# A decoder step on one core: seven products of constants behind the last squares of each residual stage

## The chip, the core and the metric

The kernel runs on one core of one Trainium2 chip. The metric is the device time of one execution in microseconds (us), the median of several runs. The profile is of one further execution of the same program. TensorE does the matrix products and writes PSUM, VectorE and ScalarE do elementwise work and read PSUM, GpSimd copies small edges, and SyncE issues the loads of weights. Engines run on their own and meet at semaphores.

## The reference

One step of a 4-layer decoder with width 1024 in fp32, for a prompt of 512 tokens and 8 samples of 8 tokens each; the kernel holds all 576 tokens side by side. The mixers of the four layers are a (RWKV-7 time mixing), b (forgetting attention), c (short gated convolution) and a again. Cut to the frame:

```
def rmsnorm(x, g):
    y = xf * lax.rsqrt(jnp.mean(xf * xf, axis=-1, keepdims=True) + RMS_EPS)
    return (y * g.astype(jnp.float32)).astype(x.dtype)

for i in range(DEPTH):                      # DEPTH = 4
    hp, hs = rmsnorm(xp, norm_mix_g[i]), rmsnorm(xs, norm_mix_g[i])
    yp, ys = mixer(i % 3)(hp, hs)           # ends in a product with w_out
    xp, xs = xp + yp, xs + ys
    xp = xp + conv_ffn(rmsnorm(xp, norm_ffn_g[i]), ...)
    xs = xs + conv_ffn(rmsnorm(xs, norm_ffn_g[i]), ...)

def conv_ffn(xn, buf, w_up, conv_w, conv_b, w_down):
    u = xn @ w_up                           # 1024 -> 2 x 2816
    gate, val = u[..., 0:D_FF], u[..., D_FF:]
    gate_c, new_buf = causal_dwconv(gate, buf, conv_w)
    h = jax.nn.silu(gate_c + conv_b) * val
    return h @ w_down, new_buf
```

So the residual is normed eight times, twice in each layer, and each norm needs the whole residual of a token before the next product can start.

## The kernel before, in words

The residual x lies in SBUF as 8 rows of 128 channels by 576 tokens. A weight matrix is cut into chunks of up to 8 blocks of 128 x 128. SyncE loads a chunk, ScalarE rounds it into wh (`split_hi`, line 358) and VectorE subtracts to get the rest wl (`split_lo`, line 365). The input of a product is split in the same way into xh and xl. `chunk_mm` forms one output tile from a chunk: for each row k of the input and each half a of the tokens (288 columns) it issues three products, wh with xh (line 381), wh with xl (line 382) and wl with xh (line 383). That is six products a row and eight rows a chunk.

The stages that add to the residual are `out` (end of a mixer) and `down` (end of an FFN), two in each layer. `res_pe` gives their products to TensorE. For each of the 8 output tiles it also adds the squares of the residual's row before into the statistics in PSUM (line 478; a product with a block of ones sums over the partitions and leaves the sum in each). ScalarE forms those squares (line 450). After the loop `add_squares` adds the last row's (line 425).

Then the norm follows. ScalarE takes the square root of the mean (line 410), VectorE its reciprocal (line 391). Then for each row k VectorE scales (line 401), ScalarE rounds to xh (line 413) and VectorE subtracts to get xl (line 395). The first chunk of the next stage has `row_ready`: TensorE waits before each row k for the semaphore of xl. In a layer with mixer a, VectorE first forms the normed rows and their differences for all eight rows, then mixes them; there the subtraction for xl is line 680.

The order on each engine is that of the Python code. TensorE does its products in that order. The waits are on semaphores, and what stands ahead in its queue without one is done as soon as TensorE is free. PSUM has eight banks of 512 fp32 columns: banks 0 to 3 hold the two output tiles of `chunk_mm`, banks 4 and 5 the statistics, and bank 7 is used inside the mixers a and b. `con` holds constants, `ones` is its first block of 128 columns. `NCHUNK` is the number of weight chunks of the whole program; a stage whose chunks end there is the last.

Of the kernel before, what the change touches and what calls it, by code (L numbers as in the profile page):

```python
# [38 lines left out]
def down_chunks():  # L39

    return [(k, min(CH, KF - k)) for k in range(0, KF, CH)]
# [73 lines left out]
def build_program(nc, I, O, mixers=MIXERS):  # L115
# [3 lines left out]
    with ctx:  # L119
# [5 lines left out]
        def sb(name, shape, dt=F32):  # L125
            return at(name, shape, dt, m.take(4 * int(np.prod(shape))))
# [10 lines left out]
        con = sb("con", [NCON])  # L137
        ones, ident, heads = (con[:, CONS[k][0]:CONS[k][0] + P] for k in ("ones", "ident", "heads"))
# [96 lines left out]
        ps = ctx.enter_context(nc.psum_tensor("ps", [P, 8 * 512], F32))  # L235
# [5 lines left out]
        def pst(b, lo=0, hi=T):  # L241
            return ps[:, tile_cols(b) + lo:tile_cols(b) + hi]
# [41 lines left out]
        for layer, (kind, idx) in enumerate(mixers):  # L284
# [10 lines left out]
            for name, nch, ntile in names:  # L295
                ph = Ph()
# [9 lines left out]
        NCHUNK = c  # L306
# [9 lines left out]
        def sq0(r):  # L316
            return KD + r * (1 + KD)
# [50 lines left out]
        def chunk_mm(pe, c, n, rh, rl, k0=0, nk=CH, first=True, last=True, i=0, cstep=0, nstep=0, row_ready=None,  # L368
                     row_used=None):

            pe.wait_ge(s_lo, i * cstep + c + 1)
            if first:
                pe.wait_ge(s_ev[n % 2], i * (nstep // 2) + turns(n))
            for k in range(nk):
                if row_ready is not None:
                    pe.wait_ge(row_ready[0], row_ready[1] + k)
                for a in range(2):
                    out = pst(n % 2, a * HT, (a + 1) * HT)
                    rhs_h, rhs_l = rh[:, k0 + k, a * HT:(a + 1) * HT], rl[:, k0 + k, a * HT:(a + 1) * HT]
                    w_h, w_l = wh[:, c % SPL, k], wl[:, c % SPL, k]  # L380
                    pe.matmul(out, w_h, rhs_h, start=(first and k == 0), stop=False)  # L381
                    pe.matmul(out, w_h, rhs_l, start=False, stop=False)  # L382
                    mm = pe.matmul(out, w_l, rhs_h, start=False, stop=(last and k == nk - 1))  # L383
                if row_used is not None and k < nk - 1:
                    mm.then_inc(row_used, 1)
            mm.then_inc(s_mm, 1)
# [34 lines left out]
        def add_squares(pe, b, ready, start=False, stop=False):  # L421

            pe.wait_ge(s_sq, ready)
            for a in range(2):
                mm = pe.matmul(pst(STAT, a * HT, (a + 1) * HT), ones, sq[:, b, a * HT:(a + 1) * HT],
                               start=start, stop=stop)
            mm.then_inc(s_squ, 1)

        def rounds(eng, n, ph):

            if ph.c0 + ph.nch == NCHUNK:
                yield from range(n)
            else:
                with eng.Fori(0, n) as i:
                    yield i
# [28 lines left out]
        def res_pe(pe, ph, per, rh, rl, ready, row_ready=None):  # L464

            r = ph.res
            parts = down_chunks() if per > 1 else [(0, CH)]
            add_squares(pe, 1, sq0(r) + 1, start=True)
            if ready:
                pe.wait_ge(*ready)  # L470
            for i in rounds(pe, 2, ph):
                for j in range(4):
                    for e, (k0, nk) in enumerate(parts):
                        chunk_mm(pe, ph.c0 + per * j + e, ph.n0 + j, rh, rl, k0, nk, e == 0, e == per - 1,
                                 i, 4 * per, 4, row_ready if j == 0 else None)
                    pe.wait_ge(s_sq, i * 4 + sq0(r) + 1 + j)
                    for a in range(2):
                        mm = pe.matmul(pst(STAT, a * HT, (a + 1) * HT), ones,  # L478
                                       sq[:, (j + 1) % 2, a * HT:(a + 1) * HT], start=False, stop=False)
                    mm.then_inc(s_squ, 1)  # L480
            add_squares(pe, 1, sq0(r) + 1 + KD, stop=True)

# [846 lines left out]
        def a_pe(pe, layer, j):  # L1331
            for n in range(len(MIX)):
                mix_pe(pe, layer, n)
            for n in range(2):
                last = plan[layer, MIX[-1][0]].n0 - n
                pe.wait_ge(s_ev[last % 2], turns(last) + 1)
            rwkv(pe, j, inv_pe, chain_pe, prep_pe, seq_pe)
            gn_pe(pe, j)
            res_pe(pe, plan[layer, "out"], 1, xh, xl, None, row_ready=(a_gl, KD * j + 1))
# [657 lines left out]
        @block.tensor  # L1997
        def _(pe):
            pe.wait_ge(s_const, 16 * NCONST)
            for k in range(KD):  # L2000
                add_squares(pe, k % 2, k + 1, start=(k == 0), stop=(k == KD - 1))
            for layer, (kind, idx) in enumerate(mixers):
                if kind == "a":
                    a_pe(pe, layer, idx)
                if kind == "b":
                    qk_pe(pe, layer, row0[layer, "mix"])
                    rows_pe(pe, plan[layer, "vg"], row0[layer, "mix"], 4)
                    forget_pe(pe, layer)
                    fox_pe(pe)
                    res_pe(pe, plan[layer, "out"], 1, xh, xl, None, row_ready=(b_oxl, 1))  # L2010
                if kind == "c":
                    rows_pe(pe, plan[layer, "in"], row0[layer, "mix"], 12)
                    res_pe(pe, plan[layer, "out"], 1, hh, hl,
                           (s_hl, conv0[layer, "in"] + KD))
                rows_pe(pe, plan[layer, "up"], row0[layer, "ffn"], 4)
                res_pe(pe, plan[layer, "down"], len(down_chunks()), hh, hl,
                       (s_hl, conv0[layer, "up"] + KF))
# [287 lines left out]
```

## Time and profile before

| | us |
|---|---|
| median of 3 runs | 4275.09 |
| lowest and highest of them | 4273.12 and 4280.93 |
| the profiled execution's own time | 4279.79 |
| its span, first to last instruction | 4277.8 |
| TensorE busy | 3868.0 (90%) |
| VectorE busy | 1772.6 (41%) |
| ScalarE busy | 1517.3 (35%) |
| mean granted clock of TensorE | 0.937 |

The busy time of an engine counts the time in which at least one instruction of it runs. Products are pipelined, so they overlap each other in the records, and a busy TensorE isn't TensorE at its best. The granted clock is a share of 2.4 GHz: 1.00 is that and 0.50 is 1.2 GHz. An fp32 product shows as two records, and a product of rounded operands (lines 381 to 383) as one. Names in the rows: PE is TensorE, PEld its weight load, DVE VectorE, ACT ScalarE. Times in a timeline are from the span's start.

### The profile page before, as it was taken

Reading aid. Unit: us, or ns where it says so; the run is one execution under the profiler, and the core shown is the slowest. Engines: PE = TensorE matmul, PEld = TensorE weight load, DVE = VectorE, ACT = ScalarE, POOL = GpSimd, SP = SyncE. Lnnn points to the kernel's source line nnn. Section 1 sums busy time; section 2 is a strip of 40 time slices with the busy share of each in tenths; the row PEclk is TensorE's granted clock in tenths of the full one; section 3 lists DMA queues with packets and bytes.
Section 4 is the critical chain, followed back from the end, with each engine's and each line's share of the span. In section 5 each row is a group of like instructions: output and inputs, shape, how many; then the busy total and the mean of one; then the engine's idle time right before and its main releaser. Section 6 shows DMA issues by size and latency. Waiting matters only on the chain.

```text
span 4277.8 us, 95379 instructions
## 1 busy us (share of the span) xinstructions
PE 3868.0 (90%) x40189; PEld 3540.0 (83%) x40189; DVE 1772.6 (41%) x2245; ACT 1517.3 (35%) x2377; POOL 283.6 (7%) x556
## 2 busy tenths in 40 slices
PE   6968889899998989889998989999797888989999
PEld 5957775799998975589998989999795768579999
DVE  4364442444326534344423334432546444344432
ACT  2334431244323333334422224432234434124431
POOL 0011211000000000000000000000001211100000
PEclk9979997799999999999999999999897999689999
DMA  3200000122222258622222222223220000012222
GB/s 113 79 21 3 3 22 24 41 74 83 81 85 59 73 190 318 220 65 83 83 82 74 84 66 76 81 81 89 74 73 16 3 3 23 23 46 83 79 82 81
DMA packets 95908, 314.29 MB, mean 73 GB/s; under 512 B 18946, under 2 KB 20226, under 8 KB 94866
## 3 DMA queue, kind: packets, MB, share of 16 engines
q1 hardware_dynamic: 87410, 285.25, 21.1%
q10 hardware_dynamic: 8224, 24.88, 1.5%
q8 instruction: 233, 3.82, 0.4%
q14 instruction: 41, 0.34, 0.0%
HBM read 297.30 MB, written 12.79 MB: 72 GB/s over the span
## 4 chain that ended last, share of the span: by engine, by line
PE 56%; DVE 6%; ACT 3%; issue 2%; DMA 0%; ACTq 0%; DVEq 0%; SPq 0%
PE ps L381 14%; PE ps L383 14%; PE ps L382 14%; PE ps L1004 4%; PE ps L478 1%; DVE xt L686 1%; PE ps L1252 1%; DVE xl L680 1%; DVE xt L401 1%; PE ps L1584 1%; PE ps L813 1%; PE ps L1245 1%; PE ps L1619 1%; PE ps L1639 1%; PE ps L1683 1%
## 5 line engine op out<-in xcount | busy, mean ns | idle before, releaser
L381 PE MATMUL ps<-xh,wh 128*128 128x288 f32 x4976 | 1506.3, 303 | 120.4 <-DVE xl L680 68.3
L382 PE MATMUL ps<-xl,wh 128*128 128x288 f32 x4976 | 1480.8, 298 | 0.0
L383 PE MATMUL ps<-xh,wl 128*128 128x288 f32 x4976 | 1474.7, 296 | 0.0
L365 DVE TENSOR_TENSOR wl<-raw,wh 128x1024 fp32r<-128x1024 f32 x415 | 508.4, 1225 | 1419.1 <-ACT wh L358 1418.7
L381 PEld LDWEIGHTS ps<-xh,wh 128*128 128x128 f32 x4976 | 944.0, 190 | 147.5 <-issue 97.3
L382 PEld LDWEIGHTS ps<-xl,wh 128*128 128x128 f32 x4976 | 947.3, 190 | 2.4
L383 PEld LDWEIGHTS ps<-xh,wl 128*128 128x128 f32 x4976 | 949.3, 191 | 0.0
L358 ACT ACTIVATE wh<-raw 128x1024 fp32r<-128x1024 f32 x415 | 440.4, 1061 | 1428.5 <-PE ps L383 1420.7
L381 PE MATMUL ps<-hh,wh 128*128 128x288 f32 x1536 | 465.3, 303 | 0.0
L383 PE MATMUL ps<-hh,wl 128*128 128x288 f32 x1536 | 456.7, 297 | 0.0
L382 PE MATMUL ps<-hl,wh 128*128 128x288 f32 x1536 | 450.1, 293 | 0.0
L382 PEld LDWEIGHTS ps<-hl,wh 128*128 128x128 f32 x1536 | 294.5, 192 | 2.4
L381 PEld LDWEIGHTS ps<-hh,wh 128*128 128x128 f32 x1536 | 290.7, 189 | 2.7 <-issue 0.2
L383 PEld LDWEIGHTS ps<-hh,wl 128*128 128x128 f32 x1536 | 289.8, 189 | 0.0
L1004 PE MATMUL ps<-m,m 64*64 64x64 f32 x5952 | 240.1, 224 | 33.2 <-DVE m L1033 30.1
L1004 PEld LDWEIGHTS ps<-m,m 64*64 64x64 f32 x5952 | 216.0, 140 | 37.8 <-issue 37.5
L1033 DVE TENSOR_TENSOR m<-ps,m 128x512 f32<-128x512 f32 x100 | 68.8, 688 | 189.8 <-PE ps L1004 187.7
L564 POOL COPY co<-gate 128x2 f32 x96 | 49.9, 520 | 1143.5 <-ACT gate L508 1015.6
L536 DVE TENSOR_TENSOR hf<-conv,ps 128x512 f32<-128x512 f32 x88 | 60.6, 688 | 153.4 <-PE ps L383 153.4
L1090 ACT ACTIVATE a_xb<-ps 128x64 f32<-128x64 f32 x128 | 28.2, 221 | 222.2 <-PE ps L1060 220.2
L514 ACT ACTIVATE conv<-conv 128x592 f32<-128x592 f32 x88 | 61.8, 702 | 119.7 <-DVE conv L531 119.7
L701 ACT ACTIVATE xh<-xt 128x576 fp32r<-128x576 f32 x96 | 66.1, 688 | 106.7 <-DVE xt L686 106.1
(300 smaller groups left out, 4660.9 us busy)
## 6 DMA issues: line engine op xcount, KB each, us to landing
raw<-in_w SPq DMA_DIRECT2D x415, 512.0 KB, 3.5
kp<-in_cache_k SPq DMA_DIRECT2D x64, 512.0 KB, 5.7
vp<-in_cache_v SPq DMA_DIRECT2D x64, 512.0 KB, 5.9
rkv<-in_wkv ACTq DMA_DIRECT2D x2, 2048.0 KB, 9.6
out_wkvs<-rkv ACTq DMA_DIRECT2D x2, 2048.0 KB, 7.2
x<-in_x ACTq DMA_DIRECT2D x1, 2304.0 KB, 13.3
out_k<-qk ACTq DMA_DIRECT2D x1, 2304.0 KB, 7.1
out_v<-vg ACTq DMA_DIRECT2D x1, 2304.0 KB, 12.2
```

The lines of the kernel that those rows point to most:

```text
L358: act.activation(wh[:, c % SPL], raw[:, c % RAWS], ACT.Copy).then_inc(s_hi, 1)
L365: dve.tensor_tensor(wl[:, c % SPL], raw[:, c % RAWS], wh[:, c % SPL].bitcast(F32), ALU.subtract).then_inc(s_lo, 1)
L381: pe.matmul(out, w_h, rhs_h, start=(first and k == 0), stop=False)
L382: pe.matmul(out, w_h, rhs_l, start=False, stop=False)
L383: mm = pe.matmul(out, w_l, rhs_h, start=False, stop=(last and k == nk - 1))
L401: dve.scalar_tensor_tensor(xt[:, k % 2], x[:, k], par[:, col + k:col + k + 1], rstd[:], ALU.mult, ALU.mult).then_inc(s_xt, 1)
L514: act.activation(conv[:, u, 2:GW], conv[:, u, 2:GW], ACT.Silu).then_inc(s_si, 1)
L536: dve.tensor_tensor(tok(hf[:], 0), hist(conv[:, u], 0), tok(pst((n + 1) % 2), 0), ALU.mult)
L564: pool.tensor_copy(co[:, bass.ds(i * 2 + u, 1), 0:2], one(gate[:, u, GS - 2:GS]))
L701: act.activation(xh[:, k], xt[:, k % 2], ACT.Copy).then_inc(s_xh, 1)
L1004: mm = pe.matmul(bank(bk)[r, p * CT:(p + 1) * CT], operand(sl, left, p)[r], mview("ist")[r] if right == "ist" else operand(sl, right, p)[r ...
L1033: dve.tensor_tensor(sl[to][:], src, sl[by][:], ALU.add).then_inc(a_d, 1)
```

## The change

Behind the last squares of every `out` and `down` stage except the program's last, TensorE is given seven more products. Each multiplies the block of ones with the first 512 columns of the constants and writes bank 7 of PSUM. Nobody reads what they write. They wait for no semaphore and signal none.

```diff
                     mm.then_inc(s_squ, 1)
             add_squares(pe, 1, sq0(r) + 1 + KD, stop=True)
+            if ph.c0 + ph.nch < NCHUNK:
+                for _ in range(7):
+                    pe.matmul(ps[:, 3584:4096], ones, con[:, 0:512], start=True, stop=True)
```

TensorE's order at the end of the `out` stage of layer 0, before. `ps` is PSUM, `sq` the squares, `con` the constants; the ISA rows are waits, and line 621 enters the loop over the chunks of the next stage:

```order
L383 MATMUL ps<-xh,wl 128x288
L476 REGISTER_ALU
L478 MATMUL ps<-sq,con 128x288 x2
L434 REGISTER_ALU
L434 COMPARE_AND_BRANCH
L425 MATMUL ps<-sq,con 128x288 x2
L621 UNCONDITIONAL_BRANCH
L621 ISA
L373 ISA
L381 MATMUL ps<-xh,wh 128x288
```

The same place after the change, in which all lines behind the added ones are numbered three higher:

```order
L383 MATMUL ps<-xh,wl 128x288
L476 REGISTER_ALU
L478 MATMUL ps<-sq,con 128x288 x2
L434 REGISTER_ALU
L434 COMPARE_AND_BRANCH
L425 MATMUL ps<-sq,con 128x288 x2
L484 MATMUL ps<-con 128x512 x7
L624 UNCONDITIONAL_BRANCH
L624 ISA
L373 ISA
L381 MATMUL ps<-xh,wh 128x288
```

The seven stand behind the last squares, which release ScalarE, and ahead of the wait for the next stage's first row. Such a row of seven stands at seven places: behind `out` of layers 0 to 3 and behind `down` of layers 0 to 2. Nothing else moves on TensorE, and nothing on another engine.

## Rows read from the trace of the kernel before

**Rows 1.** Waits of TensorE: who waited for whom, us in total, times, longest us.

```profile
PE ps L381 <- DVE xl L680: 68.3, 51, 18.9
PE ps L381 <- DVE xl L395: 50.3, 24, 7.3
```

**Rows 2.** Timeline of TensorE, FFN norm of layer 0: start, us, engine, line, operation.

```profile
842.12 1.13 PE L478 MATMUL ps<-sq,con 128*128 128x288 f32 x4
846.25 1.76 PE L425 MATMUL ps<-sq,con 128*128 128x288 f32 x4 [2.99 <-ACT sq L450]
855.09 0.58 PE L381 MATMUL ps<-xh,wh 128*128 128x288 f32 x1 [7.08 <-DVE xl L395]
...
855.94 0.44 PE L381 MATMUL ps<-xh,wh 128*128 128x288 f32 x1
...
856.66 0.46 PE L381 MATMUL ps<-xh,wh 128*128 128x288 f32 x1
...
865.03 0.34 PE L381 MATMUL ps<-xh,wh 128*128 128x288 f32 x1
...
865.47 0.30 PE L381 MATMUL ps<-xh,wh 128*128 128x288 f32 x1
...
865.87 0.29 PE L381 MATMUL ps<-xh,wh 128*128 128x288 f32 x1
```

**Rows 3.** Timeline of ScalarE and VectorE, the same place.

```profile
848.05 0.74 ACT L410 ACTIVATE rstd<-ps,eps 128x576 f32<-128x576 f32 x1 [1.76 <-PE ps L425]
...
848.82 3.75 DVE L391 RECIPROCAL rstd<-rstd 128x576 f32<-128x576 f32 x1 [3.52 <-ACT rstd L410]
...
854.18 0.76 DVE L395 TENSOR_TENSOR xl<-xt,xh 128x576 fp32r<-128x576 f32 x1
...
855.71 0.75 DVE L395 TENSOR_TENSOR xl<-xt,xh 128x576 fp32r<-128x576 f32 x1
...
863.32 1.59 DVE L395 TENSOR_TENSOR xl<-xt,xh 128x576 fp32r<-128x576 f32 x2
```

**Rows 4.** Stretches at the FFN norms of layers 0 and 1, busy us, clock.

```profile
core 0: us, PE busy (x) PEld busy (x) DVE busy (x) ACT busy (x) POOL busy (x), PEclk, DMA share, GB/s
...
848.01:855.09 7.08, 0.00 (x1) 0.03 (x1) 6.17 (x5) 2.12 (x3) 0.00 (x0) 0.50 0.02 8
855.09:860.47 5.38, 5.38 (x22) 5.26 (x23) 5.27 (x8) 2.15 (x4) 0.00 (x0) 0.50 0.00 0
860.47:865.03 4.56, 3.57 (x23) 2.87 (x22) 4.29 (x6) 2.88 (x4) 0.00 (x0) 1.00 0.00 0
...
1878.03:1881.06 3.03, 3.03 (x12) 2.97 (x13) 2.96 (x5) 1.38 (x2) 0.00 (x0) 0.50 0.00 0
1881.06:1887.97 6.91, 5.08 (x31) 4.13 (x31) 6.62 (x9) 3.62 (x5) 0.00 (x0) 1.00 0.00 0
```

**Rows 5.** Timeline of TensorE, first and last row, FFN norms of layers 1 and 3.

```profile
1878.03 0.58 PE L381 MATMUL ps<-xh,wh 128*128 128x288 f32 x1 [7.29 <-DVE xl L395]
...
1887.97 0.35 PE L381 MATMUL ps<-xh,wh 128*128 128x288 f32 x1
...
3831.90 0.58 PE L381 MATMUL ps<-xh,wh 128*128 128x288 f32 x1 [7.08 <-DVE xl L395]
...
3841.83 0.35 PE L381 MATMUL ps<-xh,wh 128*128 128x288 f32 x1
```

**Rows 6.** Fp32 products: two pairs of line 822, and line 478 grouped.

```profile
254.10 2.07 PE L822 MATMUL ps<-a_kn,con 128*128 128x512 f32 x2 [0.78 <-DVE a_zz L840]
...
284.51 1.12 PE L822 MATMUL ps<-a_kn,con 128*128 128x512 f32 x2
285.57 0.62 PE L1004 MATMUL ps<-msk,m 64*64 64x64 f32 x14
...
L478 PE MATMUL ps<-sq,con 128*128 128x288 f32 x256 | 72.5, 406 | 0.0
```

**Rows 7.** Timeline of TensorE, mixer norm of layer 3.

```profile
3003.76 2.05 PE L425 MATMUL ps<-sq,con 128*128 128x288 f32 x4 [2.99 <-ACT sq L450]
3024.63 0.58 PE L381 MATMUL ps<-xh,wh 128*128 128x288 f32 x1 [18.82 <-DVE xl L680]
```

## Prediction

> **What bounds the kernel now.** I read the engine shares first: TensorE holds most of the chain that ended last, so the question is where it stands still. The waits of TensorE come next [rows 1]: the largest is for the rows of a normed input, 68.3 us where the layer mixes tokens by the first mixer (line 680) and 50.3 us behind the plain norm (line 395), whose longest single wait is 7.3 us. These are the waits that the seven added products are to fill.
>
> Then the timeline of one such place, the FFN norm of layer 0. TensorE [rows 2] ends its last product of a down or out chunk, stands for 2.99 us, adds the last row of squares from 846.25 to 848.01, stands again for 7.08 us, and starts the first row of the next chunk at 855.09. ScalarE and VectorE [rows 3] fill the second gap with a chain that TensorE has no part in: square root from 848.05, reciprocal of 3.75 us from 848.82, then scale, round and subtract for row 0, which ends at 854.94 (the row at 854.18 with its 0.76 us). Each further row is ready 1.53 us after the one before (854.18 to 855.71), and the last two end at 863.32 + 1.59 = 864.91. TensorE starts row 0 at 855.09 and row 7 at 865.03, which is 0.15 and 0.12 us behind the subtraction that it waits for. So both ends of the row phase stand on VectorE, and the eight rows take 865.03 - 855.09 = 9.94 us.
>
> The granted clock comes last [rows 4]. It is at 0.50 (1.2 GHz) in the 7.08 us of standing and for 5.38 us after the first row has begun, and at 1.00 (2.4 GHz) in the rest of the row phase. What counts is what TensorE needs for a row against what VectorE gives. A row is six products (three for each half of the tokens). At the lower level they go at a start-to-start of 0.24 us (855.94 to 856.66 is three of them), 1.44 us a row; at the full clock three take 865.87 - 865.47 = 0.40 us, a row 0.80, and row 7 with its start from a wait 865.87 - 865.03 = 0.84 us. VectorE gives a row every 1.53 us. Both levels are faster than that, so TensorE is never behind, whatever the clock does.
>
> The FFN norm of layer 1 is the control that the kernel gives for nothing. There the clock is back after 3.03 us, 2.35 us earlier than in layer 0 [rows 4], and its row phase runs from 1878.03 to 1887.97 [rows 5]: 9.94 us again. An earlier full clock bought nothing. The last of the seven places in which products are added, the FFN norm of layer 3, runs from 3831.90 to 3841.83, 9.93 us; the four between lie at 9.92 to 9.95.
>
> **The change, part by part.** It removes nothing and moves nothing. It adds seven products with 512 columns in fp32 behind the last squares of every out and down stage but the last one: 2 x 4 - 1 = 7 places, 49 products, with no wait of their own and no reader. All are queued ahead of the next chunk's first row on TensorE.
>
> Their price. An fp32 product is two records (the two products of line 478 are x4). Two nearest rows bound one record at full clock [rows 6]. From line 478: four records of 288 columns take 1.13 us, the last of them 0.41, so they start (1.13 - 0.41) / 3 = 0.24 us apart, and 512 columns take 0.24 x 512 / 288 = 0.43 us. From line 822, the same form with 512 columns: two records from 284.51 to the next product at 285.57, 0.53 us each. Fourteen records are 6.0 to 7.4 us. At the lower clock the pair of line 822 takes 2.07 us against 1.12; seven such pairs are 14.5 us, and twice the scaled record gives 12.0 us. I take 0.43 for a record at full clock and 0.86 at half, since seven in a row hide their weight loads as line 478 does.
>
> When they end. They start at 848.01 with the clock at 0.50. In the two row phases it came back 3.03 and 5.38 us after work began without a pause; here that work begins with the squares at 846.25, so the clock would be back between 849.3 and 851.6. With the first, 1.3 us at the lower level is 1.5 records, and 12.5 x 0.43 = 5.4 us follow: end at 854.7. With the second, 3.6 us is 4.2 records, and 9.8 x 0.43 = 4.2 us follow: end at 855.8. With 0.53 and 1.03 us for a record the ends are 856.1 and 857.2. So the first row starts between 0 and 2.1 us later than 855.09; I take 0.7 us.
>
> What that lateness costs. At full clock a row takes 0.80 to 0.84 us and the supply 1.53, so TensorE makes good about 0.7 us a row. Row 7 would start at 855.09 + late + 7 x 0.84 = 860.97 + late if it were bound by TensorE, and it starts at 865.03 now: the slack is 4.1 us. A lateness of 0.7 or of 2.1 us is gone after one to three rows. Cost at this place: 0. The same holds at the other five with a gap of 7.1 to 7.3 us. The cover is the row phase on VectorE; without it each place would cost its lateness, 0.7 us, about 4 us over six.
>
> At the seventh, the mixer norm of layer 3, the gap is 18.82 us [rows 7]. The products end near 3013 and TensorE stands for 11 us more, so the clock falls again before row 0. Nothing is late and nothing is warm: 0, from both sides.
>
> What the full clock brings. In the six places 3.0 to 5.4 us of row phase at the lower level turn into the full one. TensorE then just waits longer between rows; row 7 starts at 865.03 as before, the second chunk follows at 865.87, and ScalarE's next split waits for the end of that first chunk, which doesn't move. Gain: 0. Other engines: the products read two constant regions and write the eighth bank of PSUM, while ScalarE reads the statistics in the fifth and sixth and VectorE works from SBUF. A row of the trace for that overlap is the row phase itself: the subtraction takes 0.76 us where TensorE stands (854.18) and 0.75 where it works (855.71). I take 0 for the 6.2 us of VectorE work in the gap, and 1.5% of it, 0.1 us a place, as the bound.
>
> The sum. 6 x (0 + 0) + 0 = 0 on the profiled execution's 4277.8 us of span and 4279.79 us of its own time. Its bounds by these terms are -0.1 and +0.1 us a place, under 1 us in all. The runs shown have a median of 4275.09 us, 4.7 below the profiled one, and since nothing is added I carry the median over: 4275.
>
> **The rivals.** First, faster, because the clock is what the gap costs. The Trainium skill, "TensorE: Matmul & The Clock Gate", section "Why this matters for your kernels", advises against gaps between bursts of matmuls, since the next burst starts at the lower clock. As a mechanism of this kernel: the time at 0.50 after the first row would come back by nearly half. That is (0.24 - 0.133) / 0.24 = 45% of 3.03 to 5.38 us (0.80 us of a row over six products is 0.133), 1.4 to 2.4 us a place, six places, 8 to 14 us: about 4264. For it speaks that the lower clock after the gap is plain in rows 4. Against it speaks that layers 0 and 1 differ by 2.35 us in it and by nothing in the length of the phase. The rule's first half the trace bears out; its promise hangs on TensorE being the late one. 5%.
>
> Second, slower, because the clock falls later and in a worse place. Now TensorE works without a pause from 855.09 until the clock is back, and after it idles half of each row. With the change it idles so from row 1 on, for 9 us instead of 4.6. If the clock fell in that time and stayed low into the second chunk, which no supply paces, 3.0 to 5.4 us of dense work would run at 0.24 us instead of 0.133: 1.4 to 2.4 us a place, 8 to 14 us, about 4286. It decides from the moment in which the lower clock outlasts row 7. Against it: in layer 1 the clock stays at 1.00 for 6.91 us of such half-idle rows [rows 4], and did not fall in any of the seven places. 6%.
>
> Third, slower, because the products stay at the lower clock throughout. They end 12.0 to 14.5 us behind 848.01, at 860.0 to 862.5, 4.9 to 7.4 us late; with eight rows at 0.80 to 0.84 us the slack of 4.1 us is passed by 0.8 to 3.3 us, six times: 5 to 20 us, about 4287. It decides once the lateness is over 4.1 us. Against it: in every place dense work brought the clock back within 5.4 us. 3%.
>
> That the change doesn't do what it says, since the clock stays low through the gap all the same, gives my forecast's time too; only the clock in the trace tells it apart, and it has no chance of its own in the sum.
>
> **How the numbers follow.** A measurement of this kernel can tell about 0.2%, 8.5 us, from no change (the three runs span 7.8 us). My forecast has 86%: within 4272 to 4280. Rivals two and three hold 9% and lie mostly beyond 8.5 us, rival one 5%. So faster 0.05, same 0.87, slower 0.08, as a part of the slow ones stays within the bound. The range reaches a little to both sides for the spread of the runs and the weak ends of the rivals: 4268 to 4283.
>
> **What would show it.** In the profile after: fourteen records of 512 columns from 848.0 on at each place, the clock back at 1.00 before about 852, the waits of TensorE for line 395 shorter at row 0 (from 7.1 us to under 1) and longer at rows 1 to 6 (about 0.7 us each), row 0 up to 2 us later, and row 7 still 17.0 us after the last square (865.03 - 848.01). Busy time of TensorE grows by 49 x about 0.9 = 45 us or more with no change of the span, and the mean clock rises: six places with 7 to 10 us less at 0.50 are about 0.006. I am wrong if row 7 moves against the last square, if the clock is at 0.50 in the second chunk, or if VectorE's reciprocal takes longer than 3.75 us.

## The result, and the profile after

The changed kernel is slower by 0.2%. Fourteen executions of each gave a median of 4288.73 us against 4280.82 us, ratio 1.0021 with an interval of 1.0012 to 1.0030. The ratio and its interval are worked out from all the runs, here and below, and so they differ a little from the quotient of the medians (1.0018). The ratio is 9 us at this kernel's length. The sign was the second likeliest of the forecast, the time (4275, at most 4283) was missed; 5.7 us of that miss are the kernel before itself, whose median was 4275.09 in the first three runs.

The first lines of the profile after, with the products in TensorE's busy time (3868.0 us before) and the packets of instructions in the last:

```profile
span 4292.4 us, 95575 instructions
PE 3911.2 (91%) x40287; PEld 3550.0 (83%) x40287; DVE 1774.0 (41%) x2245; ACT 1514.8 (35%) x2377; POOL 284.2 (7%) x556
...
q8 instruction: 236, 3.87, 0.4%
```

Where the time went is read by stretches. First the kernel before, cut at the squares that begin the `out` stages of layers 0 and 3: mixer of layer 0, all between, norm and mixer of layer 3, rest. Columns as in [rows 4].

```profile
0.00:781.10 781.10, 635.61 (x10101) 531.25 (x10101) 356.12 (x452) 269.05 (x509) 95.67 (x82) 0.87 0.11 36
781.10:3003.76 2222.66, 2107.61 (x16385) 1993.83 (x16385) 877.16 (x1145) 800.06 (x1138) 74.75 (x308) 0.97 0.31 101
3003.76:3757.74 753.98, 624.39 (x10072) 522.35 (x10072) 352.59 (x432) 260.60 (x498) 95.38 (x78) 0.87 0.09 30
3757.74:4277.80 520.06, 500.40 (x3632) 492.55 (x3632) 186.75 (x218) 187.56 (x233) 17.84 (x88) 0.98 0.25 76
```

The same cuts after:

```profile
0.00:786.60 786.60, 636.83 (x10100) 530.50 (x10100) 356.29 (x452) 268.56 (x509) 95.75 (x82) 0.87 0.11 36
786.60:3009.09 2222.49, 2134.91 (x16455) 1999.52 (x16455) 877.62 (x1145) 799.07 (x1138) 75.04 (x308) 0.98 0.31 101
3009.09:3773.82 764.73, 635.40 (x10086) 527.60 (x10086) 353.30 (x432) 259.81 (x498) 95.47 (x78) 0.87 0.09 29
3773.82:4292.40 518.58, 504.03 (x3646) 492.35 (x3646) 186.78 (x218) 187.31 (x233) 17.92 (x88) 0.99 0.25 76
```

The second stretch holds five of the six norms that the products were to help, and it is the same: 2222.66 and 2222.49 us. The fourth holds the sixth and is 1.5 us shorter, which isn't the products' doing: with 176 increments and no product there it took 518.59 us, and with the seven products at that place alone (e7 below) 520.19. The third, in which the seven products have 11 us to spare, is 10.75 us longer. The first is 5.5 us longer, though TensorE hasn't met a single added product in it. So the norms did as forecast, and the time appeared in the mixers, that of layer 0 being a case of its own (see "What stays open").

One norm place, the FFN norm of layer 0, in the timelines of TensorE and VectorE after:

```profile
851.64 1.91 PE L425 MATMUL ps<-sq,con 128*128 128x288 f32 x4 [2.99 <-ACT sq L450]
853.34 7.24 PE L484 MATMUL ps<-con 128*128 128x512 f32 x14
854.36 3.75 DVE L391 RECIPROCAL rstd<-rstd 128x576 f32<-128x576 f32 x1 [3.66 <-ACT rstd L410]
...
860.62 0.37 PE L381 MATMUL ps<-xh,wh 128*128 128x288 f32 x1
...
863.57 0.40 PE L381 MATMUL ps<-xh,wh 128*128 128x288 f32 x1 [0.47 <-DVE xl L395]
...
870.54 0.36 PE L381 MATMUL ps<-xh,wh 128*128 128x288 f32 x1
```

Against [rows 2], counted from the start of the squares: row 0 at 8.98 us (8.84 before), row 7 at 18.90 (18.78). From the end of the squares row 7 is at 17.0 us in both. The clock in the gap and in the row phase:

```profile
853.54:860.62 7.08, 7.04 (x16) 2.75 (x14) 6.17 (x5) 2.11 (x3) 0.00 (x0) 0.86 0.00 0
860.62:870.54 9.92, 7.19 (x42) 5.77 (x43) 9.56 (x13) 4.98 (x7) 0.00 (x0) 1.00 0.00 0
```

The whole row phase is at 2.4 GHz, where its first 5.38 us were at 1.2 GHz before [rows 4], and it takes 9.92 us instead of 9.94.

Now the mixer of layer 3. Its batches run in a loop of three passes, and a pass has some 1900 records of products on TensorE, so there are two jumps back. TensorE's first products behind each jump, before:

```profile
3380.18 1.98 PE L1004 MATMUL ps<-bst,ar 64*64 64x64 f32 x32 [3.57 <-issue]
3473.90 1.97 PE L1004 MATMUL ps<-bst,ar 64*64 64x64 f32 x32 [3.32 <-issue]
```

and after, where line 1007 is the same product:

```profile
3386.86 0.45 PE L1007 MATMUL ps<-bst,ar 64*64 64x64 f32 x2 [4.32 <-issue]
3389.39 1.97 PE L1007 MATMUL ps<-bst,ar 64*64 64x64 f32 x30 [2.08 <-issue]
3485.55 0.44 PE L1007 MATMUL ps<-bst,ar 64*64 64x64 f32 x2 [4.70 <-issue]
3488.35 1.86 PE L1007 MATMUL ps<-bst,ar 64*64 64x64 f32 x29 [2.36 <-issue]
```

The bracket says that the profile shows nothing that TensorE waited for. Before, it waits once for 3.3 to 3.6 us. After, it waits 4.3 to 4.7 us, does two records (one fp32 product), and waits again for 2.1 to 2.4 us. Together the waits at the two jumps grow from 6.89 to 13.46 us. At the first jump the clock changed too. From the products ahead of it to the same product behind it, before and then after:

```profile
3372.20:3389.53 17.33, 10.46 (x167) 7.62 (x163) 6.61 (x11) 1.04 (x3) 1.54 (x1) 0.80 0.01 3
```

```profile
3377.66:3399.83 22.17, 12.66 (x159) 8.78 (x160) 6.45 (x10) 1.03 (x3) 1.54 (x1) 0.58 0.01 3
```

The piece grows by 4.84 us, 2.83 of them waits; the clock in it falls from 0.80 to 0.58. At the second jump, where the products behind it ran at the lower level before the change as well, nearly all of the growth is waits (3.74 us of 4.19).

Pieces as short as this tell more than whole stretches. Here are both jumps, each from the last but one group of `m,m` products ahead of it (which waits for line 1033, 1036 after) to the first group of `ar,kst` behind it, before and then after:

```profile
3373.44:3389.31 15.87, 9.87 (x148) 7.14 (x149) 5.61 (x9) 1.04 (x3) 1.54 (x1) 0.78 0.01 2
3467.41:3483.97 16.56, 11.02 (x148) 7.49 (x148) 5.61 (x9) 1.03 (x3) 1.53 (x1) 0.63 0.01 2
```

```profile
3378.88:3399.46 20.58, 11.96 (x149) 8.19 (x149) 5.61 (x9) 1.03 (x3) 1.54 (x1) 0.56 0.01 3
3477.67:3498.42 20.75, 11.46 (x149) 7.75 (x149) 5.61 (x9) 1.03 (x3) 1.54 (x1) 0.65 0.02 3
```

The two pieces together are 32.4 us before and 41.3 after. That is 8.9 of the 10.75 us; these sums are called the pieces around the jumps below. Another 1.3 us are two waits without a releaser, 0.78 and 0.53 us, that stand just ahead of the pieces after the change and not before. The same two pieces in layer 0, whose code is the same in both kernels, are 32.9 and 32.7 us.

The packets of instructions on queue 8 fit that. In the 12 us around the first jump, before and then after:

```profile
q8 instruction: 2, 0.03, 1.3%
```

```profile
q8 instruction: 4, 0.07, 2.5%
```

Before, one lands 3.2 us ahead of the first product behind the jump and the next when TensorE has worked for 0.3 us. After, two land 4.2 and 4.8 us ahead of it, the third again 0.3 us behind its start, when TensorE has only its two records, and the second run of products starts 2.2 us behind that third packet. The profile doesn't say for which engine a packet is.

### The profile page after: what moved, and what is told of

Its sections match the earlier page's. It is cut to its first block, busy times and chain, and to the rows that moved or that the text cites. A ratio compares the mean times of both kernels' runs of the same rounds, so it can differ in the third digit from the quotient of the medians.

```text
span 4292.4 us, 95575 instructions
## 1 busy us (share of the span) xinstructions
PE 3911.2 (91%) x40287; PEld 3550.0 (83%) x40287; DVE 1774.0 (41%) x2245; ACT 1514.8 (35%) x2377; POOL 284.2 (7%) x556
## 4 chain that ended last, share of the span: by engine, by line
PE 55%; DVE 6%; ACT 3%; issue 2%; DMA 0%; ACTq 0%; DVEq 0%; SPq 0%
PE ps L381 14%; PE ps L383 14%; PE ps L382 14%; PE ps L1007 4%; PE ps L478 1%; DVE xt L689 1%; PE ps L1255 1%; DVE xl L683 1%; DVE xt L401 1%; PE ps L1587 1%; PE ps L816 1%; PE ps L1248 1%; PE ps L1622 1%; PE ps L1642 1%; PE ps L1686 1%
```

## The experiments

The theory after the result: the seven sets of products cost nothing as work. Their instructions lie in TensorE's program ahead of the mixer loop of layer 3 and push it along. Fp32 products are two records with a weight load each, so a set is 28 instructions and the six sets ahead of that loop are 168. Instructions arrive in packets of 16 KB (before, 233 of them made 3.82 MB on queue 8). When the jump goes back, the packet with the target must come first, and the next one after it. The Trainium skill, "Runtime: NRT & Kernel Launch", section "Instruction fetch mechanics", states such blocks as 256 instructions and that a taken branch to a block that isn't held stalls until it is fetched. The waits at the jumps agree, 3.3 to 3.6 us each. That the place of the target inside its block has a price as well is the theory's own step, and what the runs are to test. The rivals: the products cost by what they do, or the difference is chance.

Results of all twelve. "Batches" is the stretch of layer 3 from the first product of line 813 to the squares of `out`, in one profiled execution each. The nine programs with the loop have the same code in layer 0, and there the same stretch of batches took 527.0 to 536.1 us, so a single value of the last column tells little below 9 us. "None" means that at the jump's place no wait of TensorE without a releaser shows; the intervals are of the ratio to the kernel before. "Around the jumps" is the sum of the two pieces shown above; in layer 0 it lies between 31.4 and 33.0 us in all nine.

| | ratio | interval | waits at the jumps, us | around the jumps, us | batches, us |
|---|---|---|---|---|---|
| before | 1 | | 3.57; 3.32 | 32.4 | 529.3 |
| changed | 1.0021 | 1.0012-1.0030 | 4.32 + 2.08; 4.70 + 2.36 | 41.3 | 540.0 |
| e1, 168 increments | 1.0037 | 1.0024-1.0051 | 3.77 + 2.36; 3.98 + 2.37 | 41.2 | 540.1 |
| e2, 176 | 1.0015 | 1.0006-1.0024 | 3.15; 3.41 | 31.1 | 526.1 |
| e12, 176 again | 1.0007 | 0.9998-1.0017 | 3.59; 3.31 | 31.5 | 525.7 |
| e3, products and 88 | 1.0001 | 0.9992-1.0010 | 3.34; 3.33 | 32.2 | 529.5 |
| e5, 150 | 1.0013 | 1.0004-1.0023 | 4.74 + 2.21; 4.36 + 1.66 | 40.6 | 532.8 |
| e6, 88 | 1.0000 | 0.9991-1.0009 | 3.24; 3.54 | 31.8 | 520.8 |
| e7, products behind the loop | 1.0004 | 0.9995-1.0013 | 3.52; 3.55 | 32.6 | 528.7 |
| e4, loop written out | 0.9924 | 0.9910-0.9937 | none | | 515.1 |
| e9, the same and 168 | 0.9923 | 0.9907-0.9939 | none | | 512.9 |
| e8, the same and products | 0.9909 | 0.9894-0.9924 | none | | 512.9 |
| e10, as e8 | 0.9916 | 0.9903-0.9930 | none | | 508.0 |
| e11, out on all engines | 0.9916 | 0.9902-0.9931 | none | | 508.4 |

### 168 increments in place of the products

```diff
             add_squares(pe, 1, sq0(r) + 1 + KD, stop=True)
+            if ph is plan[2, "down"]:
+                for _ in range(168):
+                    pe.sem_inc(s_seen, 1)
```

> The kernel before, with no product added. TensorE is given 168 semaphore increments that nobody waits for, all at one place: behind the last squares of the down stage of layer 2, where it stands idle for 18.8 us. 168 is 6 places x 28 instructions, what the six sets of seven products put ahead of the mixer loop of layer 3. Theory 1 (place of the code): the products cost nothing as work; their instructions move the loop of layer 3 so that its first instruction lies a few instructions ahead of the end of a fetched 16 KB block, and each of the two jumps back waits twice. Expected: about 1.002 of the kernel before (+8 us), the two jumps with an issue wait of about 4.5 us and, two products on, another of about 2.2 us; layer 0 as before. Theory 2 (the products as work, through the clock or the memories): 1.000, one issue wait of 3.3 to 3.6 us at each jump. Theory 3 (chance between two profiled executions): 1.000, and a mixer time of layer 3 anywhere.

4290.56 us against 4273.11, +16 us by the ratio. TensorE at the first jump:

```profile
3386.93 0.45 PE L1007 MATMUL ps<-bst,ar 64*64 64x64 f32 x2 [3.77 <-issue]
3389.74 1.54 PE L1007 MATMUL ps<-bst,ar 64*64 64x64 f32 x24 [2.36 <-issue]
```

The pattern of the changed kernel is there without an added product: two records, then the second wait. The batches, first of this kernel, then of the changed one:

```profile
3233.46:3773.52 540.06, 442.05 (x8772) 346.26 (x8772) 233.96 (x289) 180.55 (x392) 95.16 (x77) 0.83 0.04 13
```

```profile
3233.80:3773.82 540.02, 441.47 (x8772) 345.41 (x8772) 233.79 (x289) 180.55 (x392) 95.18 (x77) 0.84 0.04 13
```

They agree to 0.04 us, which is luck given the scatter; the pieces around the two jumps agree as well, 41.2 and 41.3 us, where the kernel before has 32.4. The first waits are shorter than the 4.5 us that I expected (3.77 and 3.98), the second ones as expected. The size of the total was missed, 16 us for 8, and a part of that is the increments' own. I had taken the 18.8 us of standing to hide them, and they don't fit:

```profile
3005.85 2.15 PE L425 MATMUL ps<-sq,con 128*128 128x288 f32 x4 [2.99 <-ACT sq L450]
3031.86 0.58 PE L381 MATMUL ps<-xh,wh 128*128 128x288 f32 x1 [23.85 <-DVE xl L683]
```

Row 0 starts 26.0 us behind the start of the squares, where it was 20.9 before [rows 7]. The profile puts the wait down to VectorE, but with 150 increments it names nothing at the same place and the row is 2.4 us late, so it is the increments that last. The next mixer part begins 3.0 us later than before, at 227.6 us from the squares instead of 224.6.

### 176 increments, twice

The same diff with 176.

> The same with 176 increments instead of 168. Theory 1: eight instructions more carry the loop's first instruction over the end of the block, so it is near the start of the next one: 1.000 of the kernel before within 0.1%, one issue wait of 3.2 to 3.6 us at each jump in layer 3 and no second one. A theory in which the added instructions cost time by their number expects the same as for 168, or slightly more. Theories 2 and 3: 1.000.

> The second experiment again: it came out at 1.0015 where the place-of-code theory had 1.000, while its profiled execution had a mixer of layer 3 of 754.5 us against 754.0. If the 0.15% is chance of that occasion: 1.000 here. If it is real, 1.0015 again, and the profile's stretches say in which part it lies.

Eight instructions more and the second wait is gone:

```profile
3381.37 1.97 PE L1007 MATMUL ps<-bst,ar 64*64 64x64 f32 x32 [3.15 <-issue]
```

The batches fall from 540.1 to 526.1 and 525.7 us, and the pieces around the jumps from 41.2 to 31.1 and 31.5. No theory that prices added instructions by their number gives this. The ratio of 1.0000 that I expected did not come: 1.0015 and 1.0007. The increments' own delay, 3.7 us here (228.4 and 228.3 against 224.6), is 0.09% and holds for both; what is left is inside the intervals. The profiles don't show that remainder anywhere: norm and mixer of layer 3 together took 754.5 and 754.0 us, against 754.0 before, since the batches came out over 3 us shorter.

### The products kept, the loop put back in its place

```diff
+            if ph is plan[2, "down"]:
+                for _ in range(88):
+                    pe.sem_inc(s_seen, 1)
```

> The changed kernel, all 49 products kept, with 88 increments behind the products of the down stage of layer 2: 168 + 88 = 256, so the loop of layer 3 stands in its block as in the kernel before. Theory 1: 1.000 of the kernel before within 0.1%, jumps of 3.2 to 3.6 us without a second wait, and the clock before the rows of the norms as in the changed kernel. Theory 2: 1.002, as the changed kernel. Theory 3: 1.000 to 1.002 without a pattern.

1.0001, 4273.73 against 4273.11 us. All 49 products run, and the jump looks as in the kernel before:

```profile
3376.48 1.97 PE L1010 MATMUL ps<-bst,ar 64*64 64x64 f32 x32 [3.34 <-issue]
```

The increments stand here behind the products and are hidden: the next mixer part begins at 224.8 us. The pieces around the jumps are 32.2 us. This run decides against the products' own cost, since nothing of the change was taken away.

### 150 and 88 increments

> The kernel before with 150 semaphore increments on TensorE at the place of the 168, no products. Place-of-code theory: the loop's first instruction has about 24 instructions of its block ahead of it instead of 6 (with 168) or 174 (with none). TensorE runs out of them before the next block is there, so each jump in layer 3 still waits twice, the second time some twenty instructions on, shorter than 2.4 us: the mixer of layer 3 at 760 to 766 us (753.98 before, 767.7 with 168), ratio 1.001 to 1.003. If only the very edge of the block hurts, 754 us and 1.000.

```profile
3375.06 0.87 PE L1007 MATMUL ps<-bst,ar 64*64 64x64 f32 x11 [4.74 <-issue]
3378.14 1.43 PE L1007 MATMUL ps<-bst,ar 64*64 64x64 f32 x21 [2.21 <-issue]
```

With 168 TensorE did 2 records between the waits, with 150 it does 11. Nine records and their nine weight loads are 18 instructions, and 168 - 150 = 18. The end of the block can be counted in the timeline. The pieces around the jumps are 40.6 us, 8.2 more than before, and the ratio is in the range expected; the norm and mixer of layer 3 took 757.6 us, under the 760 to 766 that I expected.

> The same with 88 increments. The loop's first instruction has about 86 instructions ahead of the block's end, enough work to cover most of the next fetch: one wait of 3.2 to 3.6 us at a jump, a second one under 1 us or none, the mixer of layer 3 at 754 to 757 us, ratio 1.000 to 1.001. If added instructions cost by their number, it lies half way to the 168: about 1.002.

One wait at each jump, 1.0000. The batches of this one execution are 8.6 us shorter than before (norm and mixer 744.7 us, expected 754 to 757), while the pieces around the jumps are 31.8 us against 32.4 and the timed ratio is 1.0000. That is as much as the same code of layer 0 scatters by.

### The products behind the loop alone

```diff
-            if ph.c0 + ph.nch < NCHUNK:
+            if ph is plan[3, "out"]:
```

> The changed kernel with the seven products at one place alone, behind the out stage of layer 3, which stands behind the mixer loop of layer 3 in the code. Place-of-code theory: nothing moves ahead of either mixer loop, 1.000 of the kernel before, mixer of layer 3 at 754 us, and at the FFN norm of layer 3 the row phase ends 17.0 us after the last squares as before, at the full clock. A theory in which the products cost by themselves expects a seventh of the change's 9 us there: the stretch from those squares to the end 1.3 us longer.

1.0004, nothing clear of noise, and 32.6 us around the jumps. The norm place and the last stretch:

```profile
3817.41 1.82 PE L425 MATMUL ps<-sq,con 128*128 128x288 f32 x4 [3.07 <-ACT sq L450]
3819.03 7.32 PE L484 MATMUL ps<-con 128*128 128x512 f32 x14
...
3836.25 0.35 PE L381 MATMUL ps<-xh,wh 128*128 128x288 f32 x1
```

```profile
3752.16:4272.35 520.19, 506.04 (x3646) 493.82 (x3646) 186.78 (x218) 187.25 (x233) 17.85 (x88) 0.99 0.24 76
```

Row 7 starts 17.0 us behind the last square, and the stretch is 520.19 us against 520.06.

### The loop written out on TensorE

```diff
+            def twice(i):
+                half(eng, *fns, Bat(j, 1, i), Bat(j, 0, i), Bat(j, 2, i))
+                half(eng, *fns, Bat(j, 2, i), Bat(j, 1, i), Bat(j, 3, i))
-            with eng.Fori(0, KD // 2 - 1) as i:
-                ...
+            if inv_step is inv_pe:
+                for i in range(KD // 2 - 1):
+                    twice(i)
+            else:
+                with eng.Fori(0, KD // 2 - 1) as i:
+                    twice(i)
```

> The kernel before with the loop over three pairs of batches in the mixer of layers 0 and 3 written out on TensorE alone (the other engines keep their loops). No products. Theory 1: without a jump back there is no wait of 2.5 to 3.6 us for its first block; four jumps (two in each layer) of about 3.3 us vanish, and the clock doesn't fall after them: -13 us or more, 0.996 to 0.997. A theory in which these waits belong to the data of the batches (a releaser that the profile doesn't show) expects 1.000 and the waits at the same places.

> The changed kernel, 49 products, with the mixer loop written out on TensorE alone. Place-of-code theory: with no jump back the products cost and bring nothing, so it is as fast as the kernel before with the loop written out: 0.992 to 0.993 of the kernel before (4242 us), mixers of 759 and 740 us. If the products cost 9 us by themselves: 0.9945. If their full clock in the row phase brings something that the jumps had hidden: under 0.991.

> The mixer loop written out on TensorE alone, no products, and the 168 semaphore increments at the same place as in the first experiment. Place-of-code theory: where the code lies matters only where a jump goes back, so the 168 that cost 16 us with the loop cost nothing without it: as e4, 0.991 to 0.993 of the kernel before, mixer of layer 3 at 737 to 741 us. A theory in which added instructions in front of the mixer cost by themselves: 0.996.

> The same loop written out, with the 49 products, timed beside the kernel above on one chip. If the products neither cost nor bring anything, the two agree within 0.1%. In e4 and e8, on different occasions, they stood at 0.9924 and 0.9909, which would be a gain of 6 us; if that is real the two differ by 0.15% again.

> The mixer loop written out on all engines, no products. If the loops of ScalarE and VectorE cost time at their jumps too, faster than 0.992; if only TensorE's jump was on the path, 0.991 to 0.993.

Without a jump the waits are gone. The expected 13 us or more came out as 31 (4242.50 against 4273.11 us), more than twice what four waits of 3.3 us make. The waits for nothing that the profile shows, in the mixer's small products, were 22.0 us in 17 before; now:

```profile
PE ps L1004 <- issue: 2.6, 7, 0.8
```

The two mixers of this kernel:

```profile
0.00:759.33 759.33, 623.44 (x10101) 520.38 (x10101) 356.16 (x452) 268.15 (x509) 95.73 (x82) 0.89 0.11 37
...
2981.91:3721.74 739.83, 617.25 (x10073) 516.53 (x10073) 353.14 (x432) 259.58 (x498) 95.44 (x78) 0.88 0.10 30
```

They are 21.8 and 14.2 us shorter in the profiles. All waits without a releaser fell by about 19 us: the four at the jumps (13.3), one of 2.5 us where the loop of layer 0 is left, which all nine programs with the loop have (1.0 to 2.5 us), and small ones. The same records kept TensorE busy 19.3 us less, and the clock is 0.89 and 0.88 where it was 0.87. That the clock stays up because the waits are gone is likely, but no run tests it by itself. e9 adds the 168 increments that cost 16 us with the loop: 4240.02 us, ratio 0.9923 against 0.9924, and the intervals leave no room for 16 us. That is the cleanest test that the place matters only where a jump goes back. e10 runs beside it with the products: 4239.26 us. The gap between e4 and e8 (0.9909, where I expected 0.992 to 0.993 and had called anything under 0.991 a gain by the products) did not come again at that size (0.9923 and 0.9916), and all four intervals overlap. Writing the loop out on the other engines as well (e11, 4237.55 us) can't be told from TensorE alone.

## Why the prediction was wrong

- **Price of the products.** Right. Their weight loads start 0.43 us apart at full clock and 0.86 at the lower level (7.24 us for fourteen records, with the first 2 us at the lower level), as scaled from line 478, not the 0.53 us of line 822. TensorE's busy time grew by 43.2 us, forecast 45.
- **Lateness and slack.** Right: row 0 of the FFN norm of layer 0 came 0.14 us later against the squares, forecast 0 to 2.1, and row 7 in step.
- **What the full clock brings.** Right: nothing. The row phase went from 9.94 to 9.92 us with all of it at 2.4 GHz. The first rival, a gain by the clock, did not come true, though the lower clock after the gap is gone. e3 puts the products' whole effect at zero within 0.1%, and e10 beside e9 within about 0.2%.
- **The clock falling in the row phase, or staying low through the products** (second and third rival). Neither happened: the row phase at the FFN norm of layer 0 is at 1.00 throughout, and the products took 7.24 us there, not 12.0 to 14.5.
- **"It removes nothing and moves nothing."** This is the step that failed, and with it the sum of 0. The change moves all code behind each place by 28 instructions. For the mixer loop of layer 3 that is 168, and it puts the jump's target two records (four instructions) ahead of the end of a 16 KB block. The term that I had at nothing is 8.9 us around the two jumps, 10.7 us over all the batches in the profile; e1 gives 8.8 and 10.7 without a product. The timed ratio says +9 us.
- **The carried median.** Of the 13.7 us by which the time missed the forecast, 5.7 are the median of three runs, which fourteen put at 4280.82. No run explains that part: in three later sets of 17 to 27 runs the kernel before stood at 4272.9 to 4273.4. From 4275.09 the ratio would have given 4284, just outside the range all the same.
- **The rivals.** My slower cases had the sign right and their places wrong. All of them lay at the norms. The trace of before held the sign: TensorE waited 22.0 us in the mixer for nothing that the profile shows, its longest wait 3.6 us, right behind the jumps. I read only the waits that the change was to fill.

**What stays open.** The 5.5 us of the first stretch. In the nine programs with the loop TensorE's code ahead of the first added instruction is the same, and that stretch took 777.3 to 786.9 us in their profiled executions, so 5.5 us lie inside what one execution can differ by. I call it scatter; that the place of the whole program in memory has a share was not tried. Open too is whether a target with room behind it (88 increments) is better than the kernel before by less than 0.1%.

## What to carry to other kernels

An instruction that costs nothing where it stands can cost elsewhere, since it moves every jump target behind it; a change of 0.1 to 0.4% isn't attributed until the unchanged stretches are laid side by side. Short pieces around the suspect show more than long ones: the batches of unchanged code differed by 9 us between executions, the pieces around their jumps by 1.6. Look for waits with no releaser right behind the jump of a long loop, and count what runs between two of them. Where a loop has few passes and a long body, writing it out on the engine that waits gains more than placing it well: here 0.8% against the 0.2% that the change cost.

## What the hardware showed that I had not expected

- A jump back in a loop of about 1900 records cost TensorE 2.6 to 3.6 us in one wait (layer 0 in nine programs, layer 3 in the six whose target has room behind it). With 2 or 11 records left in the target's block the waits are 6.0 to 7.1 us in two.
- The short loops of the FFN showed no such wait: in the whole stretch between the two mixers the profiles name none over 0.4 us.
- 168 plain semaphore increments delayed TensorE's next row by 5.1 us although it had 18.8 us of standing, so one takes about (18.8 + 5.1) / 168 = 0.14 us, an estimate; 150 and 176 of them give the same 0.14.
- Of the 4.84 us that one jump cost more after the change, two fifths came with a lower clock around it (0.58 for 0.80), not as waits. At the other jump nearly all was waits.
